# A two-block transformer kernel: in the pooling mixer, the pooled products, a softmax and a weight split change places

## What is computed

```python
def hybrid_mixer(n, w_in, w_pool, pool_scale, w_out):
    z = n @ w_in
    u, q, k, v = jnp.split(z, [D_POOL, D_POOL + D_ATTN, D_POOL + 2 * D_ATTN], axis=-1)
    y_pool = multiscale_pool(u, w_pool, pool_scale)      # causal means of 2, 4, 8, 16 tokens, then 128x128 products
    y_attn = dilated_attention(q.reshape(hs), k.reshape(hs), v.reshape(hs)).reshape(B, S, D_ATTN)   # 8 heads of 64
    return jnp.concatenate([y_pool, y_attn], axis=-1) @ w_out
...
h = h + gt2 * hybrid_mixer(n, w_in[l], w_pool[l], pool_scale[l], w_out[l])
```

## Time and profile before

| | |
|---|---|
| median of 3 runs | 836.94 us (832.35, 836.94, 839.76) |
| the profiled execution | 835.18 us, span 833.0 us |
| mean granted PE clock | 0.952 |
| PE busy | 745.0 us (89%) |
| DVE busy, ACT busy, POOL busy | 545.7 us, 366.7 us, 121.2 us |

### The profile page before, as it was taken

One profiled execution on the slowest core, in us unless ns is written; L12 is line 12 of the kernel. 1 busy time (PEld: TensorE's weight loads), 2 busy tenths in 40 slices (PEclk: granted clock), 3 DMA queues, 4 the chain that ended last, 5 costly groups with the idle time before them and its releaser, 6 DMA issues.

```text
span 833.0 us, 14911 instructions
## 1 busy us (share of the span) xinstructions
PE 745.0 (89%) x6112; PEld 695.8 (84%) x6112; DVE 545.7 (66%) x782; ACT 366.7 (44%) x558; POOL 121.2 (15%) x77
## 2 busy tenths in 40 slices
PE   5699999999978976889999999994999977999984
PEld 4489999999957966779999999993887767888884
DVE  3589968877756345567478556557588756678741
ACT  3253433434325344435443343354465564665532
POOL 0051113223333521240004000002000000000000
PEclk9799999999978998898999999998899999999998
DMA  9986898777648882354568565552133324433201
GB/s 311 349 265 229 278 362 285 230 243 265 219 161 279 281 263 68 101 165 141 201 212 256 188 196 163 195 188 90 58 119 103 105 99 152 152 103 106 97 2 50
DMA packets 132455, 152.64 MB, mean 183 GB/s; under 512 B 2616, under 2 KB 126268, under 8 KB 132284
## 3 DMA queue, kind: packets, MB, share of 16 engines
q1 hardware_dynamic: 132324, 152.01, 56.3%
q10 hardware_dynamic: 88, 0.02, 0.0%
HBM read 150.97 MB, written 1.05 MB: 182 GB/s over the span
## 4 chain that ended last, share of the span: by engine, by line
PE 37%; DVE 8%; ACT 7%; issue 3%; POOL 0%; DVEq 0%; ACTq 0%; POOLq 0%
PE sc L1206 5%; PE sc L1208 5%; PE acc L1206 5%; PE sc L1207 5%; PE acc L1208 5%; PE acc L1207 5%; ACT prob L658 3%; DVE wlo L831 2%; ACT whi L568 2%; PE stat L1217 1%; PE acc L1432 1%; PE acc L1434 1%; PE acc L1433 1%; DVE rstd L851 1%; ACT probT L665 1%
## 5 line engine op out<-in xcount | busy, mean ns | idle before, releaser
L831 DVE TENSOR_TENSOR wlo<-raw,whi 128x2048 fp32r<-128x2048 f32 x105 | 259.2, 2472 | 133.4 <-ACT whi L568 133.2
L568 ACT ACTIVATE whi<-raw 128x2048 fp32r<-128x2048 f32 x105 | 200.2, 1907 | 76.0 <-PE sc L1208 63.4
L1206 PE MATMUL sc<-nhi,whi 128*128 128x256 f32 x704 | 200.7, 285 | 6.0 <-DVE nlo L870 4.1
L1207 PE MATMUL sc<-nlo,whi 128*128 128x256 f32 x704 | 199.4, 283 | 0.0
L1208 PE MATMUL sc<-nhi,wlo 128*128 128x256 f32 x704 | 199.3, 283 | 0.0
L1206 PEld LDWEIGHTS sc<-nhi,whi 128*128 128x128 f32 x704 | 134.7, 191 | 7.4 <-issue 4.5
L1207 PEld LDWEIGHTS sc<-nlo,whi 128*128 128x128 f32 x704 | 136.2, 193 | 0.0
L1208 PEld LDWEIGHTS sc<-nhi,wlo 128*128 128x128 f32 x704 | 135.1, 192 | 0.0
L1206 PE MATMUL acc<-nhi,whi 128*128 128x256 f32 x376 | 113.8, 303 | 18.2 <-DVE nlo L870 10.7
L1207 PE MATMUL acc<-nlo,whi 128*128 128x256 f32 x376 | 108.3, 288 | 0.0
L1208 PE MATMUL acc<-nhi,wlo 128*128 128x256 f32 x376 | 108.1, 287 | 0.0
(11 more groups left out here) (184 smaller groups left out, 1149.7 us busy)
## 6 DMA issues: line engine op xcount, KB each, us to landing
ada<-in_w_ada_dram SPq DMA_DIRECT2D x28, 1024.0 KB, 5.2
raw<-in_w_gate_dram SPq DMA_DIRECT2D x22, 1024.0 KB, 5.8
raw<-in_w_up_dram SPq DMA_DIRECT2D x22, 1024.0 KB, 5.5
raw<-in_w_down_dram SPq DMA_DIRECT2D x22, 1024.0 KB, 4.8
raw<-in_w_out_dram SPq DMA_DIRECT2D x12, 1024.0 KB, 5.3
raw<-in_w_in_b_dram SPq DMA_DIRECT2D x10, 1024.0 KB, 5.1
raw<-in_w_in_a_dram SPq DMA_DIRECT2D x9, 1024.0 KB, 5.2
raw<-in_w_in_dram SPq DMA_DIRECT2D x8, 1024.0 KB, 7.6
```

Source lines behind the costliest of these rows:

```text
L568: nc.scalar.activation(whi[:, u % NS], raw[:, u % NS], ACT.Copy).then_inc(hi_done, 1)
L831: nc.vector.tensor_tensor(wlo[:, u % NS], raw[:, u % NS], whi[:, u % NS].bitcast(F32), ALU.subtract).then_inc(lo_done, 1)
L1206: mm(to, stat_hi, mov_hi, start=first, stop=False, skip_group_check=True)
L1207: mm(to, stat_hi, mov_lo, start=False, stop=False, skip_group_check=True)
```

## The change

Three kinds of edit. In the list, W0 and W1 go ahead of V1 (so the three jobs W0, W1, V1 swap accumulator banks: W0 and V1 are in `acc0`, W1 in `acc1`). ACT treats the step pair V1, SC0 in the pool mixer as it treats Z, SC elsewhere: exponentials of heads 0 and 1, then the eviction of V1, then heads 2 and 3, then the high part of the unit after next; and DVE divides heads 0 and 1 before it takes the maximum of head 2. The split of unit 43 (the columns of OUT2), which stood behind TPV0 on ACT and DVE, goes behind the softmax of SC1. Finally a one-element `Exp` (`load_exp`) is put ahead of each of the three mixers, which is where the compiler then sets the table load that stood ahead of each mixer's first exponential.

```diff
-                     "MOD26", "ROW28", "V1", "SC0", "W0", "W1", "Q1", "TPV0", "SC1", "OUTA", "TPV1", "OUTB", "ROW29",
+                     "MOD26", "ROW28", "W0", "W1", "V1", "SC0", "Q1", "TPV0", "SC1", "OUTA", "TPV1", "OUTB", "ROW29",
...
+            def load_exp():
+
+                nc.scalar.activation(junk[:, 6:7], tiny[:, 0:1], ACT.Exp)
...
-                if kind == "Z" or (kind == "Q" and st["next"]["kind"] == "TPV"):
+                if kind == "Z" or (kind == "Q" and st["next"]["kind"] == "TPV") or (kind == "V" and st["next"]["kind"] == "SC"):
                     return
...
-                        if before["kind"] == "Z":
+                        if before["kind"] in ("Z", "V"):
                             softmax(st, (0, 1))
                             job(before)
                             softmax(st, (2, 3))
                             st["after"] = before["u"]
-                            if st["next"]["kind"] != "Q":
+                            if before["kind"] == "V" or st["next"]["kind"] != "Q":
                                 high(before["u"] + NS)
                         else:
                             softmax(st)
+                            high(st["late"] + NS)
                     elif st["kind"] == "TPV":
                         early = before["kind"] == "Q"
                         outputs(st, early)
-                        if early:
+                        if early and name == "pool":
+                            st["next"]["late"] = before["u"]
+                        elif early:
                             high(before["u"] + NS)
...
             norm_high(1)
+            load_exp()
             high(FFN_UNIT[0] + 3 * FB + 2)
             mixer("pool")
...
-                        if before["kind"] == "Z":
+                        if before["kind"] in ("Z", "V"):
                             divide(st, 0)
                             divide(st, 1)
-                            gate(before)
+                            if before["kind"] == "Z":
+                                gate(before)
                             masked_max(st, 2)
...
-                        low(before["u"] + NS) if before["kind"] in ("Z", "V") else None
+                        low((before if before["kind"] in ("Z", "V") else query)["u"] + NS)
                     elif kind == "TPV":
                         outputs(st)
-                        if name == "pool" and before["kind"] == "Q":
-                            low(before["u"] + NS)
```

More of the change, by code:

```diff
@@ L685, in mixer @@
                             high(before["after"] + NS)
-                    if st["kind"] == "Z":
+                    if st["kind"] == "Z" or st["kind"] == "V" and st["next"]["kind"] == "SC":
                         pass
```

## The result

The changed kernel takes 829.9 us (median of 20 runs, 826.6 to 834.4) against 836.3 us (20 runs, 830.0 to 842.0): ratio 0.9933, 95% interval 0.9916 to 0.995. That is 5.6 us won by the ratio (4.2 to 7.0). The time lies inside the forecast range of 824.5 to 832 us, but less was won than the 9.2 us forecast, and less than 1%, to which the prediction had given 0.41.

What follows compares the result with a forecast made beforehand. PE, busy 89% of the span, was taken as the bound, with only its pauses and slow stretches to win. 8.9 + 2.5 = 11.4 us, less 2.2 for the clock, gave 836.94 - 9.2 = 827.7 us, range 824.5 to 832.

Steps and rivals of the forecast that it cites:

- the sum: Pool mixer total: 8.9 us plus 2.5 us won, together 11.4, less 2.2 for the clock: 9.2 us won.
- the second rival: First softmax later than thought, by blocked divisions or another slow stretch: 1.5 to 3.5 us less won, some 830.2 us; chance 0.22.
- Part 1: W0 and W1 moved ahead: the 7.46 us wait and slow clock behind it go, first TPV0 product 8.9 us earlier.
- Part 2: Unit 43 behind SC1's softmax: 2.66 us wait goes, 4.7 us wait added, first TPV1 product 11.4 us earlier in all.
- Part 3: Slow clock behind the new gap ahead of TPV1, lasting 4.5 to 7 us: 1.1 to 3.4 us lost, 2.2 taken.
- Part 4: Things worth nothing: moving the table loads wins and costs 0; later loads of units 45 and 46 are covered.
- a gain taken back by something fixed in time: Rival: something such as a transfer for the output projection takes the gain back, 836.9 us; chance 0.05.
- a clock that stays down: Rival: clock falls in the new gap and stays at 0.50 over the dense output projection, 849 us; chance 0.05.

Runs made afterwards that it cites:

- experiment 10: Changed kernel with ACT's eviction of V1 again ahead of the exponentials of heads 0 and 1: ratio 0.9954 to the kernel before, stage 72.64 us.
- both fillings: Unread matmuls put into PE's gaps: 28 in the changed kernel (ratio 0.9876, stage 67.99 us), 60 and 18 in the kernel before (0.9982, 76.42 us).
- experiment 4: Changed kernel without the three one-element exponentials that load the table early: ratio 0.9924 to the kernel before, stage 71.40 us.
- experiment 1: Changed kernel with the split of unit 43 put back behind TPV0 on ACT and DVE: ratio 0.9892 to the kernel before, stage 70.75 us.
- experiment 2: Kernel before with only the split of unit 43 moved behind the softmax of SC1: ratio 1.0064, stage 81.29 us.
- experiment 9: Changed kernel with unit 43 back behind TPV0 and 18 unread matmuls ahead of the scores of head 6: ratio 0.9905 to the kernel before, stage 69.88 us.
- experiment 7: Changed kernel with only unit 43's high part (ACT) back behind TPV0, plus 20 unread matmuls in the remaining gap: ratio 0.9870 to the kernel before, stage 66.51 us.
- experiment 6: Changed kernel with only unit 43's high part (ACT) back behind TPV0, low part (DVE) left behind the softmax: ratio 0.9865 to the kernel before, stage 66.29 us.

## Why the prediction was partly right

The time fell into the forecast range, but 3.6 us less were won than forecast. In the stage 1.3 us are missing, mainly because the clock's price was set 1.2 us too low. The other 2.3 us are missing outside the stage, and no term of the sum covers them. The 829.9 us are close to the 830.2 us of the second rival, a late first softmax. That is luck: the softmax was late by 0.2 us.

**Part 1** held. The pooled products start 1.0 us after ROW28, scores 0 and 1 and V1 follow them without a wait, ACT has copied W1 out of its bank at 303.74 us, 4.6 us before Q1 asks for it, and Q1's projection runs through at clock 1.00. The first product of TPV0 was won 8.7 us instead of 8.9 us. The division beside the masks took 1.33 us, between the two rows I had weighed. The 0.2 us are found in the masks: from the start of head 2's to the end of head 3's POOL took 4.8 us (305.85 to 310.63), where I had taken twice 2.27 us.

**Part 2** held in its instructions: 11.5 us at the first product of TPV1, against 11.4 us in the sum. The wait there was 3.77 us and not 4.7 us, because the transposes of TPV1 end at 326.2 us and not at 325.0, in part as the second of them waits 0.37 us for DVE's division; the product itself was where I had put it.

**Part 3**, "Between these ends I take the middle, 2.2 us lost", is the step that failed in size. Filling the gap gives back 3.4 us, the upper end of my own bounds, but not by the way I had reckoned it: not 7 us all over dense work, but some 10 us, of which about two thirds cost time (3.4 us against half of 10.2). I took a length of 4.5 to 7 us for the slow stretch, from the two in the trace. It was about 10 us in the three profiles of kernels with this gap and this order (the changed one twice, the one without the early load) and in that of experiment 10. The kernel before and the one with unit 43 back had stretches of about 7 us. Why this one lasted longer the runs don't show.

With both fillings the stage can be split. At held clock the instructions take 76.42 us before and 67.99 us after: 8.4 us won. The clock took 2.9 us before and takes 3.4 us after: 0.5 us more. The difference is the 7.9 us of the two profiles. The sum had 11.4 us, which holds the 2.9 us of the kernel before, so it had 8.5 us for the instructions, and these were right. It took off 2.2 instead of 3.4 us for the new slow stretch.

**The rest** of the shortfall, from 7.9 us in the stage to 5.6 us by the ratio (4.2 to 7.0), is not in the stage. The spans of the two profiled executions differ by 4.4 us (833.04 against 828.66): 7.9 us are won in the stage, 0.3 us lost ahead of ROW28 and 3.2 us behind the second feed-forward, where PE is busy 3.6 us longer over the same matmuls. Whether the change has a part in this stays open. Against it stands that this part took 459.5 and 462.7 us in the two profiles of the changed kernel, and 456.3 us in that of experiment 4, which lacks only the early table loads and whose ratio is the same within the noise.

**The judgement on the parts** was wrong in one point that the total hides: I counted the move of unit 43 as a gain that pays for its gap ("11.4 us won in all", less 2.2 for the clock). Experiments 1, 2 and 9 speak against it: 0.6 us lost in the stage on the changed kernel, 2.0 us on the kernel before. By the times it is clear of noise only in experiment 2 that the move gains nothing. The pooled products and the split softmax make the whole gain, and 1.25 us of it is the order of V1's eviction and the first exponentials. The move is worth 1.9 us at held clock, and the clock costs 3.4 us with it and 0.9 us without. The Trainium skill, page "TensorE: Matmul & The Clock Gate", section "Why this matters for your kernels", had spoken against just such a wait, with its warning of idle gaps between bursts of matmuls. The trace agrees: filling the gap of 3.77 us gave back 3.4 us.

**Part 4** held: the table load is worth 0, though by experiment 4 with only 0.21 us to spare in the pool mixer. No wait of PE of 1.2 us or more in the stage is put down to a transfer. The rivals of a gain taken back by something fixed in time and of a clock that stays down were not seen.

## What to carry to other kernels

Before moving an instruction off one wait, see which queue it enters next and how long the matmul engine then stands. A gap that lies under a softmax may cost less, slow clock included, than a shorter chain whose gap lies right ahead of dense matmuls. Where a split is two instructions on two engines, each may have its own best place: here the high part ahead of the exponentials and the low part behind the divisions gave 0.9865 where moving both gave 0.9933. And matmuls that nobody reads, put into a gap, measure the clock's share of a loss, as long as they end inside the gap: 28 of them did in 3.8 us, 20 in 2.0 us delayed the next product by 0.3 us.

## What was unexpected

The price of a gap can't be read from its length alone. In the places of the experiments the granted clock stayed at 1.00 behind waits of 1.80, 1.97 and 1.98 us. It fell for about 7 us behind 2.60 and 2.66 us, for about 10 us behind 3.77 us, and once (experiment 2) for some 14 us. But other waits in the same twelve profiles break this order. The wait of 4.09 us ahead of the second feed-forward goes with a slow stretch of about 7 us in ten profiles, and of 3.4 us in two (experiments 7 and 9). One of 2.68 us near 252 us, the same in every kernel, goes with a slow stretch of about 7 us in ten profiles and with none in two (experiments 1 and 10):

```profile
251.00:262.00 11.00, 8.65 (x58) 8.38 (x62) 8.10 (x19) 7.62 (x12) 0.00 (x0) 0.69 0.85 271
250.00:262.00 12.00, 10.19 (x89) 9.39 (x90) 9.11 (x19) 9.37 (x13) 1.49 (x1) 1.00 0.73 233
```

The first row is the changed kernel, the second experiment 1. What decides it these runs don't show. The wait of 4.09 us was in the trace of the kernel before too (at 376.73 us), and the prediction, which took the slow stretch from two gaps, had not looked at it.

A division of two times 128 by 128 and 128 by 256 elements on DVE took 0.55 us with POOL idle and up to 1.5 us beside POOL's masks. The place of the mask matters: the same division took 1.50 us in the changed kernel and 1.06 us in experiment 6, where it came a little later against the mask.
